# Both MLP products as seven products of half-size blocks instead of eight

## What is computed

```
def _mlp(h, w1, b1, w2, b2):
    return jnp.square(jax.nn.relu(h @ w1 + b1)) @ w2 + b2
xl = _layernorm(DEEPNORM_ALPHA * xl + mod_l[2] * mix_l, ln_post_g[l, 0], ln_post_b[l, 0])
hl2 = _modulate(xl, mod_l[3], mod_l[4])
xl = _layernorm(DEEPNORM_ALPHA * xl + mod_l[5] * _mlp(hl2, ...), ln_post_g[l, 1], ln_post_b[l, 1])
```

## Time and profile before

| | |
|---|---|
| median of 3 runs | 3239.68 us (3237.44 to 3240.63) |
| profiled execution, span | 3243.6 us |
| TensorE (PE) busy | 3095.1 us, 95% |
| weight loads (PEld) | 2552.5 us, 79% |
| VectorE (DVE) | 1789.1 us, 55% |
| ScalarE (ACT) | 631.1 us, 19% |
| GpSimd (POOL) | 326.7 us, 10% |
| DMA | 366 MB, mean 113 GB/s |

### The profile page before, as it was taken

The page is one execution under the profiler, slowest core; times in us unless marked ns, Lnnn a source line. Parts: engine busy times, 40 slices in busy tenths (PEclk is TensorE's granted clock), DMA queues, the critical chain, the costliest instruction groups (busy, mean ns, idle before and its releaser), DMA issues.

```text
span 3243.6 us, 35976 instructions
## 1 busy us (share of the span) xinstructions
PE 3095.1 (95%) x14584; PEld 2552.5 (79%) x14584; DVE 1789.1 (55%) x2617; ACT 631.1 (19%) x1181; POOL 326.7 (10%) x498
## 2 busy tenths in 40 slices
PE   6999999999996889989999999999999899999997
PEld 3888888888884678868788788888888788888886
DVE  4831133112222878856777756666557556666556
ACT  2421000111112555542212211111110111111110
POOL 0323011100001222202201000000001000000000
PEclk8999999999998999989999999999999999999999
DMA  6742233333335535448847312122115211221111
GB/s 225 233 128 83 76 104 116 118 109 109 127 111 155 171 126 180 136 145 239 225 143 237 108 52 65 49 65 64 47 53 175 88 55 56 72 65 62 47 32 65
DMA packets 264697, 366.39 MB, mean 113 GB/s; under 512 B 16451, under 2 KB 180563, under 8 KB 263126
## 3 DMA queue, kind: packets, MB, share of 16 engines
q1 hardware_dynamic: 202422, 181.08, 18.4%
q0 software_dynamic: 48752, 151.56, 14.2%
q10 hardware_dynamic: 13360, 31.46, 3.0%
HBM read 257.08 MB, written 106.96 MB: 112 GB/s over the span
## 4 chain that ended last, share of the span: by engine, by line
PE 61%; DVE 3%; DMA 2%; issue 1%; ACT 1%; SPq 0%; POOL 0%; DVEq 0%; ACTq 0%; POOLq 0%
PE mix_bank L1168 7%; PE mix_bank L1169 7%; PE mix_bank L1170 7%; PE mix_bank L1150 7%; PE mix_bank L1152 7%; PE mix_bank L1151 7%; PE mix_bank L1883 3%; PE mix_bank L1099 2%; PE mix_bank L1101 2%; PE mix_bank L1100 2%; PE mix_bank L1822 2%; PE mix_bank L130 1%; PE mix_bank L132 1%; PE mix_bank L131 1%; PE mix_bank L1827 1%
## 5 line engine op out<-in xcount | busy, mean ns | idle before, releaser
L1150 PE MATMUL mix_bank<-tail_h2h,tail_w1h 128*128 128x512 f32 x1024 | 399.7, 390 | 5.5 <-DVE tail_w1l L916 5.5
L130 PE MATMUL head_bank<-head_hTh,head_wh 128*128 128x512 f32 x1024 | 401.6, 392 | 3.1 <-DVE head_hTl L547 2.3
L1168 PE MATMUL mix_bank<-tail_w2h,tail_ah 128*128 128x512 f32 x1024 | 399.5, 390 | 4.0 <-DVE tail_acc L946 4.0
L1169 PE MATMUL mix_bank<-tail_w2l,tail_ah 128*128 128x512 f32 x1024 | 399.3, 390 | 0.0
L131 PE MATMUL head_bank<-head_hTl,head_wh 128*128 128x512 f32 x1024 | 399.3, 390 | 0.0
L1151 PE MATMUL mix_bank<-tail_h2l,tail_w1h 128*128 128x512 f32 x1024 | 399.2, 390 | 0.0
L132 PE MATMUL head_bank<-head_hTh,head_wl 128*128 128x512 f32 x1024 | 399.1, 390 | 0.0
L1170 PE MATMUL mix_bank<-tail_w2h,tail_al 128*128 128x512 f32 x1024 | 399.1, 390 | 0.0
L1152 PE MATMUL mix_bank<-tail_h2h,tail_w1l 128*128 128x512 f32 x1024 | 399.1, 390 | 0.0
L555 DVE CAST head_wh<-head_raw 128x1024 fp32r<-128x1024 f32 x64 | 44.5, 695 | 547.9 <-PE head_bank L132 415.9
L948 DVE TENSOR_TENSOR tail_acc<-tail_acc,mix_bank 128x512 f32<-128x512 f32 x416 | 275.5, 684 | 118.6 <-PE mix_bank L1170 116.4
(11 more groups left out here) (244 smaller groups left out, 4717.8 us busy)
## 6 DMA issues: line engine op xcount, KB each, us to landing
tail_raw<-in_w SPq DMA_DIRECT2D x128, 512.0 KB, 4.0
head_raw<-in_w_in SPq DMA_DIRECT2D x64, 512.0 KB, 4.2
scratch_proj<-head_stage POOLq DMA_DIRECT2D x128, 256.0 KB, 2.7
head_x<-in_w_ada ACTq DMA_DIRECT2D x8, 2048.0 KB, 10.2
mix_gates<-scratch_proj POOLq DMA_DIRECT2D x32, 512.0 KB, 7.5
head_wa<-in_w_ada SPq DMA_DIRECT2D x8, 1024.0 KB, 9.4
mix_dec<-scratch_proj SPq DMA_DIRECT2D x32, 256.0 KB, 4.5
scratch_dft_a<-mix_fa POOLq DMA_DIRECT2D x32, 256.0 KB, 4.2
```

Source lines behind the costliest of these rows:

```text
L130: nc.tensor.matmul(out, wh, xh, start=(k == 0), stop=False)
L1150: nc.tensor.matmul(U[2 * e + c][:], w1h[:, e, k, :], hT[0][k // 4][:, k % 4, cs], start=(k == 0), stop=False)
L1168: nc.tensor.matmul(V[n % 4][:], ah[z][:, ts], w2h[z][:, cs], start=(first and z == strips[0]), stop=False)
L1169: nc.tensor.matmul(V[n % 4][:], ah[z][:, ts], w2l[z][:, cs], start=False, stop=False)
```

## The change

In place of eight block products, both products of the MLP are formed from seven products of half-size blocks, with sums and differences of blocks as operands.

The up product covers one half of the tokens per 16 units (`NU` = 32, `UH` = 16). A unit is 256 hidden channels x 1024 tokens. Its seven products of 128 channels x 512 tokens take 4 x 3 matmuls each. The seven token-side operands (`oph`, `opl`, 128x2048) stay in SBUF for 16 units. Three of them are blocks of h; four are block sums that POOL makes (`mix`) from h stored in memory (`h2f`) by ACT's queue, and stores (`h2t`). The seven weight operands of a unit come from `raw1` by four DVE operations (`mixed`, `low_w`), ACT's cast (`high_w`) and DVE's difference (`low_w`). Running sums stay in PSUM. ACT copies three intermediate states to `e` (`kept`), DVE adds three banks to them (`gathered`), ACT squares (`squared`), POOL forms the four sums of activations (`paired`), and SP stores seven pieces of a unit in `a2` in memory.

The down product runs after the whole up product, not interleaved with it: 16 steps `v`, of 256 tokens (times two block rows) and one block of 1024 hidden channels, seven products with 2 x 4 x 3 matmuls each. `a2` is loaded (`load_a`, 512 KB), cast by ACT (`high_a`) and its low part formed by DVE (`low_a`). The w2 operands change with every second `v`: 1 MB loads, ACT's cast (`high_op`), POOL's low part (`low_op`). The sums of w2 blocks (`w2t`) are made by 16 further mixes of POOL; together with the four of the second half of h they are one mix a unit in units 0 to 19. w2 is no longer multiplied by `mod5`; the finished sums are (`complete`). POOL scales the residual rows in memory (`keep_left`), two rows a unit in units 20 to 24 and one in units 25 to 30.

Cast work of the weights moves from DVE to ACT. The split of h, `rows_back`, `h1h` and `h1l` go away.

The core of the diff:

```
+    def ordered(n):
+        turns = [(0, 0)]
+        for u in range(n):
+            turns += [(u, i) for i in (1, 2, 3, 4)]
+            turns += [(u + 1, 0)] if u + 1 < n else []
+            turns += [(u, 5), (u, 6)]
+        return turns
...
     def scalar(act):
...
             if j == NTILE - 3:
-                evict_h(2, 3, KD)
+                high_op(0, 1)
+                for p in range(2):
+                    high_w(p)
+                evict_h(2, 3, 6)
+                for p in range(2, LOOK):
+                    high_w(p)
+                high_op(0, 2)
+                evict_h(2, 6, KD)
+                high_op(0, 3)
...
+        def kept(p):
+            u, i = up_order[p]
+            n = (0, 2, 1)[i]
...
+            if i == 0 and u >= 2:
+                act.wait_ge(st_e[u % 2], 16 * 7 * (u // 2))
+            act.wait_ge(up_s, p + 1)
+            nc.scalar.copy(e[u % 2][n][:], (Z if i == 1 else X)[u % 2][:]).then_inc(snap, 1)
...
+        def up(p):
+            u, i = up_order[p]
+            pe.wait_ge(w_lo, p + 1)
...
+            for k in range(4):
+                nc.tensor.matmul(out[:], wh[p % 7][:, k, :], oph[i][:, k, :], start=(k == 0 and i in (0, 1, 3)), stop=False, skip_group_check=True)
+                nc.tensor.matmul(out[:], wh[p % 7][:, k, :], opl[i][:, k, :], start=False, stop=False, skip_group_check=True)
+                last = nc.tensor.matmul(out[:], wl[p % 7][:, k, :], oph[i][:, k, :], start=False, stop=(k == 3), skip_group_check=True)
+            last.then_inc(up_s, 1)
...
     def gpsimd(pool):
...
+        def mix(q):
+            m = cm[:].rearrange("p i n -> p (i n)")
+            b11, b12, b21, b22 = (m[:, n * 512:(n + 1) * 512] for n in range(4))
...
+            pool.wait_ge(ld_cm, 32 * (q + 1))
+            nc.gpsimd.tensor_tensor(ct[:, 0], b12, b11, ALU.subtract).then_inc(mix_s, 1)
+            pool.wait_ge(mix_s, 4 * q + 1)
+            nc.gpsimd.tensor_tensor(b12, b22, b12, ALU.subtract).then_inc(mix_s, 1)
+            nc.gpsimd.tensor_tensor(ct[:, 1], b22, ct[:, 0], ALU.subtract).then_inc(mix_s, 1)
+            pool.wait_ge(mix_s, 4 * q + 3)
+            nc.gpsimd.tensor_tensor(b21, b21, ct[:, 1], ALU.subtract).then_inc(mix_s, 1)
+            pool.dma_start(dst[0:2].rearrange("o p n -> p o n"), ct[:]).then_inc(st_cm, 16)
+            pool.wait_ge(mix_s, 4 * q + 4)
+            pool.dma_start(dst[2:4].rearrange("o p n -> p o n"), m[:, 512:1536].rearrange("p (o n) -> p o n", o=2)).then_inc(st_cm, 16)
...
+        for j in range(NTILE):
+            keep_rows(j)
...
+            for q in {9: (0,), 10: (1, 2), 11: (3,)}.get(j, ()):
+                load_mix(q)
+                mix(q)
+            if j == 13:
+                low_op(0, 2)
+                low_op(0, 3)
+            if j == 14:
+                low_op(0, 4)
+        low_op(0, 5)
+        low_op(0, 6)
+        for u in range(NU):
+            jobs = [u + 4] if u < 20 else [2 * (u - 20), 2 * (u - 20) + 1] if u < 25 else [u - 15] if u < 31 else []
+            if u < 20:
+                load_mix(u + 4)
+            elif jobs:
+                load_row(jobs[0])
+            if u == UH:
+                low_op(1, 1)
+                low_op(1, 4)
+            if u:
+                paired(u - 1)
+            if u == UH:
+                low_op(1, 6)
+            if u < 20:
+                mix(u + 4)
+            for n in (jobs if u >= 20 else ()):
+                if n != jobs[0]:
+                    load_row(n)
+                keep_left(n)
```

`load_mix` waits for both stores of the mix before it, `load_row` for the store of the row before it, and `paired(u)` for the last square of unit u (it makes four additions of 128x512). SP's `load_h(0, 1)` waits for all four mixes of the first half. At the end of DVE's program:

```
+            down_turn(p)
+            if down_order[p] == (NV - 1, 5):
+                for x in finals(NV - 1)[0:2]:
+                    complete(*x)
+                    statistics(*x)
+        done = finals(NV - 1)
+        result(*done[0])
+        complete(*done[2])
+        statistics(*done[2])
+        result(*done[1])
+        complete(*done[3])
+        statistics(*done[3])
+        result(*done[2])
+        result(*done[3])
```

912 lines of the change are left out of this document (590 added, 322 removed).

## The result

The changed kernel took 3283.3 us in the median of four runs (3279.7 to 3285.8) against 3239.7 for the kernel before: a ratio of 1.0131, interval 1.0117 to 1.0145. It is **slower by 1.3%**, 43.5 us; the forecast was 3212. It was the quickest of its four runs, while the 3243.6 us profiled before lie above that kernel's median; so the account covers 34.3 of the 43.5 us, and no step stands for the other 9.

A forecast was written before the change was run, and what follows sets the result against it. The MLP was taken as bound by TensorE. Savings of 174.1 and 20.3 us against losses of 42, 15, 13, 62, 5, 14 and 20, less 4, gave -27.4: 3239.7 to 3212 us, range 3140 to 3320.

The forecast's parts named there:

- Part 1: Both products: one matmul in eight removed, -174.1 us, and the starvations at the start of a half gone, -20.3 us.
- Part 2: Start of the up product: TensorE waits for four serial mixes and ScalarE's eviction, +42 us (25 to 65).
- Part 3: Units of the up product: POOL's turns exceed TensorE's 19.05 us; +15, +13 and +62, less 4 us.
- The rows' term: Units 20 to 24: POOL handles two rows each, turns of 31.5 us against 19.05, +62 us.
- lookahead: Units with two rows: lookahead gives back 4 us once.
- Part 4: Between and in the down product: operands reloaded at two borders, +5 us (0 to 15); late sums, +14.
- the 13 of the low parts: Unit 16: POOL also makes three low parts of 128x2048, +13 us (4 to 25).
- the +14: Down product, seven odd v's: POOL's low parts and DVE's need the same lock, sums late, +14 us (0 to 40).
- Part 5: End, after the last matmul: four tiles are completed there, +20 us (15 to 25).
- (b): Rival, units 0 to 19: POOL's turn, lock plus landing wait, passes 21.2 us; slower, 3275 to 3295 us; chance 0.41.
- (a): Rival, whole kernel: TensorE bound throughout, POOL's lateness mostly absorbed; times under 3175 us; chance 0.17.
- faster: Whole kernel: faster than before by over 0.2%, chance 0.52.

The follow-up runs named there:

- start: Changed kernel with ScalarE's and VectorE's work for the first unit moved out of the tile loop to behind it: 3264.6 us, ratio 1.0072.
- halfmix: Changed kernel with each of the four additions forming a block sum of the second weight matrix done on 256 of 512 columns: 3268.4 us.
- seam2: Changed kernel, between the two products: activation and w2 loads issued ahead of unit 30's stores, w2 block 0 made before the third activations: 3273.8 us.
- early: all2 with the seven border loads of operand blocks issued once the old block's last product is over, meant ahead of all stores: 3216.5 us.
- all2: Changed kernel with all order repairs (start, border, seam, VectorE's sums before statistics) and two row buffers together: 3213.6 us, ratio 0.9914.
- border2: Changed kernel with border loads and stores issued before the next weights, GpSimd's block 1 low part earlier, block 0's parts one product later: 3268.5 us.

## Why the prediction was wrong, step by step

**Part 1** was right: 768 matmuls less at 0.2267 us, and the starvations of before gone.

**Part 2, the start**, was right in its mechanism and place (the gap ended by ScalarE's eviction, behind four serial mixes) and 11 short: 53.5 against 42, within its bounds of 25 to 65. TensorE's 33.26 is near what was forecast (36.8), partly by luck: the first mix's loads were issued 8 us sooner than supposed, the mixes followed each other by 23.3, 22.6 and 15.7 us in place of 18.0, and the 1 MB load took 6.2 in place of 9.4. Missed was the second gap, 11.94 us at 1855.40, in which VectorE's rows of the last tile came late. The run start shows that part of it was order alone: 19 us.

**Part 3** was right at its core. A turn of POOL in a mixing unit was forecast at 19.8 and measured at 19.8 in units 3 to 6; halfmix shows that it is what binds. That it is equal to a tenth is luck, as the parts cancel: the wait for the last store was 4.05 for 3.1, the issues 2.9 for 2.6, and the eight additions with their gaps 12.8 for 14.1. Of these, contention made 2.5 us, as forecast (2.4), but not for the reason given: an add that meets a running operation of 0.69 four times in ten would wait 0.14 on average, not 0.3. In the trace the two engines take turns, and six of the eight additions waited. The adds beside VectorE took 1.62 to 1.74 as in the earlier trace rows; the Trainium skill's exclusive lock ("SBUF — State Buffer", SBUF: two separate sides) agrees with these rows. The low parts of 128x2048, taken at 4.1 by a slope, took 4.80 in the mean and 4.50 to 4.89 at the border; that is nearer to the 4.5 that the Trainium skill states ("GPSIMD Engine Reference", Performance versus the Vector engine). The rows' term was 62 for a turn of 31.5; the first turn was 30.91 and the mean 28.22, so +45.8, and -5.3 of lookahead: 18 too much, mostly since landings of 2.7 and 3.0 us followed one another where I had 3.1 and 5.1, and since the four sums took 5.2 in most of these turns where I had 6.9 with contention.

**Part 4 is the step that failed**: "Operands reloaded at the two borders: +5 (0 to 15; a 1 MB load, cast and split, 14 us, against five products of 2.72)". It cost 44.4 at the first border (with the 13 of the low parts counted there), and some 30 of the 56.6 at the second. The arithmetic of 14 us supposed that each load is issued when its block is free and each cast made when its load has landed. In the runs neither holds: SyncE issued the loads behind stores that wait for POOL's sums and behind other 1 MB loads, and ScalarE and VectorE, serving in order, held the weights' parts and the snapshots behind the cast that waited. Block 6 was free at 2193.3, its load issued 32.6 us later (9.7 of them before the cast of block 2, the rest in the queue) and its high part done at 2234.98, 41.7 us in all with the low part still to come, in place of 14. By the runs, order accounts for 17.5 of the border's 41.7 us and GpSimd's mixes and low parts for 7.0; the cause of the last 17 stays open. The prediction did ask what is queued behind a waiting instruction at the start, where ScalarE stands ahead of the transposes, and did not ask it again at the borders.

Of the second product the forecast was wrong in place: the low parts of the odd v's cost nothing, as TensorE was busy for 100.00 of 100 us with low parts at 4.8 us beside it; the +14 there was nothing. Lost were the gap of 17.07 at the seam (SyncE and ScalarE again, by seam2), 8.34 behind it, and 11.7 and 8.65 where VectorE finishes rows, 45.8 in all. The other 10.8 I put down to the clock: behind five of these gaps (17.07, 8.34, 4.25, 3.36 and 5.29) the granted clock was 0.50 to 0.52, and each costs about the 2.3 of the earlier trace rows. The gap of 8.34 is the mechanism that the +14 was for, in another place: two low parts on GpSimd, and beside them two operations of VectorE that take 2.29 and 1.22 us undisturbed. No run moved these low parts, so that is read from the trace alone.

```profile
2612.07 12.13 POOL L1585 TENSOR_TENSOR tail_opl<-tail_op,tail_oph 128x2048 fp32r<-128x2048 f32 x2
...
2614.31 5.53 DVE L1056 TENSOR_TENSOR tail_opl<-tail_op,tail_oph 128x2048 fp32r<-128x2048 f32 x1
2619.76 5.51 DVE L1096 TENSOR_TENSOR tail_al<-tail_a,tail_ah 128x1024 fp32r<-128x1024 f32 x1
```

**Part 5** was right in its chain: 16.6 for 20. From the last matmul to VectorE's last operation it was 22.8 us for 24.5. What was taken off was misread: the operation in the earlier trace rows is not VectorE's last, which ended at 3232.35, 7.2 us behind the last matmul and not 4.5:

```profile
3231.07 1.28 DVE L964 SCALAR_TENSOR_TENSOR tail_acc<-tail_acc,mix_t_rstd,tail_raw 128x1024 f32<-128x1024 f32 x1
```

**The rivals.** (b) came true in its sign and, by luck, in its time (3275 to 3295 held 3283), but not in its mechanism: in the units with a mix the turn was never 21.2, but for the border's two. (a) fell at the rows and the start. The answer "faster" fell with one term of 5 us, bounded at 15, in whose two places about 31 us (44.4 less the 13) and 30 us (17.07 + 8.34 and the clock's 4.6) were lost, while the terms that I called the largest were good to 18.

## What to carry to other kernels

When operands change at a border, don't compare the chain of one block with the compute beside it; write down, for each in-order queue (SyncE's issues, ScalarE's and VectorE's casts), what stands ahead of each load and each cast there, and what that waits for. A load that is free to go should not stand behind a store that waits for another engine, unless something waits for that store sooner (early); and a cast that may wait should stand behind the copies and weights that the next product needs: repairs of order and one more row buffer, with no arithmetic changed, turned +1.3% into -0.9% (all2). A serial chain on one engine with a landing in every link can eat a quarter of what one matmul in eight saves (the rows, 41 of 174 us; half of it gone with a second buffer).

## What the runs showed of the hardware

What an engine pays beside the other goes by the length of the other's instruction, so VectorE mostly paid more: in border2 its operation of 0.69 us took 5.03, beside a low part on GpSimd that ran from 2206.11 for 4.82. The two, VectorE's first:

```profile
2206.46 5.03 DVE L1076 TENSOR_TENSOR tail_wl<-tail_raw,tail_wh 128x512 fp32r<-128x512 f32 x1
...
2206.11 4.82 POOL L1593 TENSOR_TENSOR tail_opl<-tail_op,tail_oph 128x2048 fp32r<-128x2048 f32 x1 [4.10 <-ACT tail_oph L1256]
```

A GpSimd addition beside VectorE's short operations pays 0.3 to 0.5 us a time (1.27 to 1.30 alone, 1.62 to 1.74 beside VectorE); at 2220.32 in the changed kernel one took 3.31, beside a low part of VectorE's that ran from 2219.13 for 3.37. Undisturbed, an addition of half the columns took 0.73 in halfmix in place of 1.27, so by the two some 0.2 us of it are fixed. And the bandwidth was not the limit: at the seven products' 250 GB/s (share 0.80) units ran at full clock with TensorE 94 us in 100 busy. The landing of POOL's stores, 4.05 us there for the 3.1 of the earlier trace rows, was part of the turn that binds.
